# A two-layer sequence trunk on one Trainium2 core: the output gate moved into the final product, forget gates in pairs, GLA three slots earlier, weight sums on VectorE

## The reference, cut to what matters

```python
# x: (1, 2048, 1024) float32; layer 0 is S5 + sliding-window attention, layer 1 is gated linear attention (GLA)
# layer 0, end:
a_out = g * sigmoid(g @ w_glu + b_glu) * silu(g_a);  b_out = swa(q, k, v) * silu(g_b)
x = x + concat(a_out, b_out) @ ev_w_out
# layer 1:
h = rmsnorm(x, norm_w[1]);  q, k, v, r, a_lr = split(h @ od_w_in)          # 512, 512, 1024, 1024, 16 columns
log_a = log_sigmoid(a_lr @ w_a2 + b_a) / 16                                # the forget gates
o = gla(q, k, v, log_a)                                                    # 4 heads, chunks of 64, a state per head
c_out = rmsnorm_per_head(o) * norm_w * silu(r)                             # silu(r) is the output gate
x = x + c_out @ od_w_out;  return rmsnorm(x, final_norm)
```

## Time and profile before

| | us |
|---|---|
| median of 3 runs | 1678.32 (1676.89 to 1682.54) |
| the profiled execution, its own time | 1679.81 |
| its span, first to last instruction | 1677.7 |
| TensorE busy | 1598.3 (95%) |
| VectorE busy | 976.1 (58%) |
| ScalarE busy | 750.2 (45%) |
| GpSimd busy | 448.7 (27%) |
| mean granted TensorE clock | 0.987 |

### The profile page before, as it was taken

One profiled execution on the slowest core, in us unless ns is written; L12 is line 12 of the kernel. 1 busy time (PEld: TensorE's weight loads), 2 busy tenths in 40 slices (PEclk: granted clock), 3 DMA queues, 4 the chain that ended last, 5 costly groups with the idle time before them and its releaser, 6 DMA issues.

```text
span 1677.7 us, 23100 instructions
## 1 busy us (share of the span) xinstructions
PE 1598.3 (95%) x7626; PEld 1287.5 (77%) x7626; DVE 976.1 (58%) x1751; ACT 750.2 (45%) x1824; POOL 448.7 (27%) x646
## 2 busy tenths in 40 slices
PE   5999999999999989999889999996999999989998
PEld 4777788777777668888667888885788888868886
DVE  6744545667676563324476565777665666765443
ACT  6522334666666563334344343445443334442221
POOL 3883000000000341200275434345134343300110
PEclk9999999999999999999999999998999999999999
DMA  5566544455444766224367444355244343476663
GB/s 217 147 179 188 157 151 134 144 169 150 150 139 131 198 188 242 101 96 143 118 202 251 158 124 153 123 189 188 92 156 152 122 161 117 134 250 205 188 190 112
DMA packets 251388, 268.71 MB, mean 160 GB/s; under 512 B 53992, under 2 KB 186760, under 8 KB 251272
## 3 DMA queue, kind: packets, MB, share of 16 engines
q1 hardware_dynamic: 248616, 265.58, 50.5%
q10 hardware_dynamic: 2656, 1.67, 0.4%
HBM read 164.24 MB, written 102.96 MB: 159 GB/s over the span
## 4 chain that ended last, share of the span: by engine, by line
PE 71%; DVE 11%; ACT 5%; issue 5%; DMA 4%; POOL 3%; SPq 1%; DVEq 0%; ACTq 0%; POOLq 0%
PE bank L1225 22%; PE bank L2565 10%; PE bank L2623 10%; PE bank L2749 8%; PE score_banks L2565 4%; PE score_banks L2749 2%; DVE odd_stage L2300 2%; PE score_banks L1281 1%; DVE ht_lo L2242 1%; PE bank L1308 1%; DMA odd_gl_in<-scr_heads 1%; PE bank L1262 1%; DVE odd_w_lo_S L2242 1%; PE score_banks L2667 1%; PE bank L2689 1%
## 5 line engine op out<-in xcount | busy, mean ns | idle before, releaser
L1225 PE MATMUL bank<-ht_hi,ev_w_hi 128*128 128x512 f32 x576 | 239.9, 416 | 2.4 <-DVE ht_lo L937 2.4
L1225 PE MATMUL bank<-ht_hi,ev_w_lo 128*128 128x512 f32 x576 | 226.8, 394 | 0.0
L1225 PE MATMUL bank<-ht_lo,ev_w_hi 128*128 128x512 f32 x576 | 226.6, 393 | 0.0
L1225 PEld LDWEIGHTS bank<-ht_hi,ev_w_hi 128*128 128x128 f32 x576 | 109.0, 189 | 38.7 <-issue 17.1
L1225 PEld LDWEIGHTS bank<-ht_lo,ev_w_hi 128*128 128x128 f32 x576 | 108.9, 189 | 24.9
L2565 PE MATMUL bank<-ht_hi 128*128 128x512 f32 x288 | 120.1, 417 | 5.8 <-issue 5.8
L1225 PEld LDWEIGHTS bank<-ht_hi,ev_w_lo 128*128 128x128 f32 x576 | 109.2, 190 | 19.6
L712 POOL TENSOR_TENSOR ht_lo_raw<-ht_lo_raw,glu_g_first 128x512 f32<-128x512 f32 x4 | 6.4, 1642 | 415.9 <-DMA ht_lo_raw<-scr_gate_a 409.7
L2565 PE MATMUL bank<-ht_lo,ht_hi 128*128 128x512 f32 x288 | 113.2, 393 | 0.0
L2565 PE MATMUL bank<-ht_hi,ht_lo 128*128 128x512 f32 x288 | 112.7, 391 | 0.0
L2135 ACT ACTIVATE odd_gl_o<-bank 128x256 f32<-128x256 f32 x64 | 24.7, 385 | 168.6 <-DVE odd_gl_state L2361 156.0
(11 more groups left out here) (374 smaller groups left out, 4263.4 us busy)
## 6 DMA issues: line engine op xcount, KB each, us to landing
odd_w_raw<-od_w_in SPq DMA_DIRECT2D x24, 1024.0 KB, 5.8
odd_gl_in<-scr_heads SPq DMA_DIRECT2D x32, 640.0 KB, 4.8
scr_heads<-odd_stage SPq DMA_DIRECT2D x64, 256.0 KB, 6.4
ev_w_raw<-ev_w_in SPq DMA_DIRECT2D x17, 512.0 KB, 6.0
ev_s_cos_sin<-scr_s_cos_sin SPq DMA_DIRECT2D x32, 256.0 KB
odd_xo_sum<-x SPq DMA_DIRECT2D x16, 512.0 KB, 4.7
scr_x<-odd_xo_sum SPq DMA_DIRECT2D x16, 512.0 KB, 3.0
scr_gla_mix<-odd_gl_out SPq DMA_DIRECT2D x32, 256.0 KB, 2.3
```

Of the source, the lines that this page charges most:

```text
L1225: mm = pe.matmul(acc[n % 3], w[j][:, k, :], h[:, k, t], start=(k == 0 and r == 0), stop=(k == KT - 1 and r == 2))
```

## The change

The silu of r leaves the slots: its columns are stored raw, and the gate is formed in the final product, for each tile two tanh of 128x512 on ScalarE into free PSUM banks, and two more operations on VectorE behind the present one. GLA starts three slots earlier in both halves, forget gates come two in a slot. The sums of the weights move to VectorE, as do the subtractions of T3 and T4 in the middle. At the seam between the layers and in the GLU stage loads, casts and waits are reordered.

```diff
-    GLA_AT = (17, 64)
-    GATE_AT = (4, 51)
+    GLA_AT = (14, 61)
+    GATE_AT = (3, 51)
-        return [8 * half + s - at_ for half, at_ in enumerate(GATE_AT) if 0 <= s - at_ < 8]
+        return [8 * half + 2 * (s - at_) + n for half, at_ in enumerate(GATE_AT) if 0 <= s - at_ < 4 for n in range(2)]
+    m_th = [(bank[6], bank[7]), (bank[2], bank[3])]
...
     def sync(sp):
             if i == 0:                      # load_x4; in the change "if i == 1"
                 sp.wait_ge(hb_summed, 4 * N_TB)
-        load_att(0)
         load_wo(0)
         load_wo(1)
...
         load_wo(2)
         load_g(3)
+        load_att(0)
...
-            for k in gates_at(s - 2):
+            for k in gates_at(s - 1):
...
     def gpsimd(pool):
         gate_g(1)
         gate_g(2)
-        gate_att(0)
         gate_g(3)
+        gate_att(0)
...
-        for o in S_ORDER:
-            weight_sum(0, o)
-            if it + 1 < N_IT:
-                for o in {1: ("S1", "S2", "S4"), 2: ("S3",)}.get(j, ()):
-                    weight_sum(it + 1, o)
-            for o in H_SPLIT_AT.get(s, ()):
-                if o in H_LO_POOL:
-                    lower_second(o)
...
     def scalar(act):
-            if i == 11:
+            if i == 13:
                 upper_att(0)
-            if i in (5, 7, 9, 11, 13):
-                upper_wo((i - 5) // 2)
+            if i in (6, 8, 10, 12, 14):
+                upper_wo((i - 6) // 2)
...
         for m in range(NT):
+            if m == NT - 1:
+                split(0, "A11")
             if m:
                 upper_out(m - 1)
             if m == NT - 1:
-                split(0, "A11")
+                split(0, "S2")
...
+        def mix_tanh(t):
+            act.wait_ge(mix_in[j], mix_in_0[j] + 32 * (t // 2 + 1))
+            (waits for the last GLA work at t = 0 and 1, for mul_done of tile t - 2 later)
+            for h in range(2):
+                s.activation(m_th[j][h], m_sil[j][:, 4 * h:4 * h + 4], ACT.Tanh, scale=0.5).then_inc(tanh_done, 1)
...
-            (silu_tanh of four roles in the slots of is_r)
+            if s_ == 94: mix_tanh(0)
+            if s_ == 95: split_mix(0)
+            if s_ == 96: mix_tanh(1)
+            (in the final loop: if t + 2 < NT: mix_tanh(t + 2), ahead of the squares)
...
     def vector(dve):
-            if i == 12:
+            if i == 14:
                 lower_att(0)
-            if i in (6, 8, 10, 12, 14):
-                lower_wo((i - 6) // 2)
+            if i in (7, 9, 11, 13, 15):
+                lower_wo((i - 7) // 2)
...
         split(0, "A11")
+        dve.wait_ge(wo_free, wo_free_0 + 2)
+        weight_sum(0, "S1"); weight_sum(0, "S2"); weight_sum(0, "S4")
         residual(NT - 1)
         sum_first("T4")
+        split(0, "S2")
         lower_first("T2")
         normed_out(NT - 1)
-        split(0, "S2")
-        lower_first("B21")
+        weight_sum(0, "S3")
         split(0, "A12")
         split(0, "S3")
+        lower_first("B21")
         lower_first("T4")
...
         def gated(t):
-            v.scalar_tensor_tensor(m_on[j][:], m_on[j][:], 0.5, m_sil[j][:], ALU.mult, ALU.mult).then_inc(mul_done, 1)
+            (the same, then_inc(half_done, 1); then for each half h, when its tanh is done:)
+                rows = m_on[j][:, 4 * h:4 * h + 4]
+                v.scalar_tensor_tensor(rows, m_th[j][h], 1.0, rows, ALU.add, ALU.mult)    # the last one: mul_done
...
             (slots: gate_log now ahead of advance; silu gone; prepare(0) waits for hb_summed)
             if step(s + 1) is not None:
                 mask(step(s + 1))
+            if it + 1 < N_IT:
+                for o in {1: ("S1", "S2", "S4"), 2: ("S3",)}.get(j, ()):
+                    weight_sum(it + 1, o)
             for o in W_SPLIT_AT[j]:
                 (split)
             for o in H_SPLIT_AT.get(s, ()):
-                if o in H_LO_DVE:
-                    lower_second(o)
+                lower_second(o)
...
     def tensor(pe):                         # out_products
             if m % 4 == 0:
                 pe.wait_ge(mix_lo_done, 4 * GLU_AT.index(m // 4) + 4)
-                pe.wait_ge(att_lo_done, m // 4 + 1)
...
+                if m % 4 == 0 and k == 4:
+                    pe.wait_ge(att_lo_done, m // 4 + 1)
```

More of the change, by code:

```diff
@@ L1483, in gates_output_odd @@
     turned_at = (raw_hi[:, 0:4, cols(1)], raw_hi[:, 4:8, cols(1)])
-    tb_in = [at(f"hb_in{j}", (20, 4)[j], [P, 4, BLK // 2]) for j in range(2)]
+    tb_in = [at(f"hb_in{j}", (20, 6)[j], [P, 4, BLK // 2]) for j in range(2)]
     tb_out = [at(f"hb_out{j}", 24 + 4 * j, [P, 4, BLK // 2]) for j in range(2)]
@@ L1800, in sync @@
             before = it - 1
-            if j == 3 and it < N_IT and not is_r(it):
+            if j == 3 and it < N_IT:
                 store_out(it, "C11")
             if j == 0 and before >= 0:
-                for role in (("C11",) if is_r(before) else ("C21", "C22")):
-                    store_out(before, role)
+                store_out(before, "C21")
+                store_out(before, "C22")
             if j == 1 and before >= 0:
-                store_out(before, "C22" if is_r(before) else "C12")
-            if j == 2 and is_r(before) and s < N_SLOT:
-                store_out(before, "C21")
                 store_out(before, "C12")
@@ L1878, in gpsimd @@
         gate_g(2)
+        gate_g(3)
         gate_att(0)
-        gate_g(3)
-        for m in range(NT):
+        for m in range(NT - 1):
             inverse_out(m)
@@ L2242, in split, with weight_sum @@
             v.tensor_tensor(w_lo[o], w_from[o], w_hi[o].bitcast(F32), ALU.subtract).then_inc(w_ready, 1)
+        def weight_sum(i, o):
+            prev = i - 1
+            if o == "S1":
+                dve.wait_ge(w_in[i % 2], 16 * (i // 2 + 1))
+                if i:
+                    dve.wait_ge(w_ready, w_ready_0 + 1 + w_no(prev, "S1"))
+                v.tensor_tensor(w_from["S1"], w_from["A21"], w_from["A22"], ALU.add).then_inc(s_added, 1)
+            if o == "S2":
+                if i:
+                    dve.wait_ge(p_done, product_no(prev, "S2"))
+                dve.wait_ge(s_added, s_no(i, "S1"))
+                v.tensor_tensor(w_from["S2"], w_from["S1"], w_from["A11"], ALU.subtract).then_inc(s_added, 1)
+            if o == "S4":
+                if i:
+                    dve.wait_ge(w_ready, w_ready_0 + 1 + w_no(prev, "S4"))
+                dve.wait_ge(s_added, s_no(i, "S2"))
+                v.tensor_tensor(w_from["S4"], w_from["A12"], w_from["S2"], ALU.subtract).then_inc(s_added, 1)
+            if o == "S3":
+                if i:
+                    dve.wait_ge(p_done, product_no(prev, "S3"))
+                v.tensor_tensor(w_from["S3"], w_from["A11"], w_from["A21"], ALU.subtract).then_inc(s_added, 1)
         def sum_first(o):
@@ L2300, in combine @@
             v.tensor_tensor(*ops, ALU.add).then_inc(ev_done, 1)
-        def silu(it, role):
-            dve.wait_ge(tanh_done, sil_no(it, role) + 1)
-            v.scalar_tensor_tensor(out_of[role], tanh[:], 1.0, out_of[role], ALU.add, ALU.mult).then_inc(sil_done, 1)
         def gate_min(k):
@@ L2463, in gated @@
             dve.wait_ge(mix_in[j], mix_in_0[j] + 32 * (t // 2 + 1))
-            v.scalar_tensor_tensor(m_on[j][:], m_on[j][:], 0.5, m_sil[j][:], ALU.mult, ALU.mult).then_inc(mul_done, 1)
+            halved = v.scalar_tensor_tensor(m_on[j][:], m_on[j][:], 0.5, m_sil[j][:], ALU.mult, ALU.mult)
+            halved.then_inc(half_done, 1)
+            dve.wait_ge(half_done, t + 1)
+            for h in range(2):
+                dve.wait_ge(tanh_done, 2 * t + h + 1)
+                rows = m_on[j][:, 4 * h:4 * h + 4]
+                part = v.scalar_tensor_tensor(rows, m_th[j][h].rearrange("p (k t) -> p k t", k=4), 1.0, rows, ALU.add, ALU.mult)
+            part.then_inc(mul_done, 1)
         def lower(t):
@@ L2482, in vector @@
                         take_low(half, k)
+            for k in gates_at(s - 1):
+                gate_log(k)
             if s and step(s - 1) is not None:
@@ L2488, in vector @@
                 prepare(step(s + 2) // 2)
-            if j == 0 and is_r(it - 1):
-                silu(it - 1, "C22")
-            if j == 1 and is_r(it - 1):
-                silu(it - 1, "C21")
             if even(step(s + 3)):
@@ L2503, in vector @@
                     split(it + 1, o)
-            if j == 1 and is_r(it - 1):
-                silu(it - 1, "C12")
-            if j == 3 and is_r(it):
-                silu(it, "C11")
             if s == 1:
```

107 lines of the change are left out of this document (35 added, 72 removed).

## The result

The changed kernel takes 1662.55 us (median of six executions, 1659.37 to 1671.97), the one before beside it 1678.34: 15.8 us less, ratio 0.9903, 95% interval 0.9879 to 0.9927. The sign was right; the forecast was 1646, and 1662.55 lies just outside its range. Half of the 32 us did not come. The profiled execution took 1660.8 (span 1659.0).

The account below looks back on a forecast made before the run. TensorE, busy 95% of the span, was taken as the bound, with only idle and lower-clock time to win; 7.5 + 7.5 + 5.0 + 7.0 − 1.0 + 0.5 + 5.5 = 32 us gave 1646 us, range 1632 to 1662 (8 in 10).

Parts of the forecast that it names:

- The start of GLA waits on the first x4 load as before; 0.5 of 1.6. Bounds 0 and 1.6.: Start of GLA: TensorE's 1.6 us wait stays mostly as it was, with 0.5 us gained.
- The forget gates: Gates in pairs: TensorE waits 5.5 us against 4.6 for gate stores, a loss of 1 us; bounds −6 and +4.
- it0 to it5: First product matmul of iteration 0 to that of iteration 5 (rest of seam, gates, GLA start): forecast −5.4 us.
- The seam's second half: Seam between the layers, behind the first product: the 2.0 us wait on S2 goes, plus 2.3 of clock.
- The GLU stage: GLU stage: TensorE's 5.8 us wait for g goes, with half the clock's 3.4; 7.5 us gained, bounds 3 and 9.
- What is late next: `gate_g(3)` [...] and `gate_att(0)`: GLU stage: the operations late next; gate_att(0) is awaited only at the fifth k of the first out product.
- The middle: Slots 46 to 50: norm not awaited, no silu, but VectorE falls behind with the pieces; 7 us gained, bounds 2 and 15.
- The slots: Second half's slots: sums on VectorE cost nothing, VectorE reaches advance earlier, norm waits mostly go; 5.0 us, bounds 0 and 5.7.
- Shifting GLA by three slots also swaps which half has its exponentials in odd slots; I give that nothing: GLA in the slots: the swap of odd and even slots between the halves counted at nothing.
- rival (3): Slots: VectorE's sums hold up GLA, directly or through GpSimd's inverse, adding 64 us; 1722 us, chance 0.04.
- The last seam: Last seam and final product: GLA no longer reaches in, gated(0) starts at once; 5.5 us gained, bounds 2 and 8.
- Rival (1): Seams only: reordered seams and the end return 19.5 us, slots and middle give nothing; 1659 us, chance 0.17.

Follow-up runs that it names:

- run 5: Changed kernel with the store of C21 of iteration 13 issued ahead of the 1 MB load of weights in slot 56; 1654.2 us, ratio 0.9860.
- run 2: Changed kernel with the first GLA at slot 17 again and the first half's forget gates one in a slot (4 to 11); 1659.3 us, ratio 0.9885.
- run 1: Changed kernel with the first GLA beginning at slot 17 again instead of 14, the second staying at 61; 1669.5 us, ratio 0.9933.
- run 3: Changed kernel, GLA at (14, 61), with only one pair of forget gates in the first half and two in the second; 1658.9 us, ratio 0.9874.
- run 10: Changed kernel with the second x4 load of the first GLA issued ahead of the 1 MB load of weights in slot 12; 1656.3 us, ratio 0.9859.
- best_a: Changed kernel with GLA at (15, 61), single first-half gates in slots 3 to 10, and the edits of run 5 and run 7; 1650.6 us, ratio 0.9821.
- run 7: Changed kernel with GpSimd's first attention product (gate_att(0)) waiting until VectorE has made the last low part of g; 1658.9 us, ratio 0.9885.
- run 8: Kernel before with its output gate (tanh on ScalarE, product on VectorE) left out, raw products stored; 1669.5 us, ratio 0.9951.
- run 4: Changed kernel with the sums of weights S1 to S4 back on GpSimd in the places of the kernel before; 1666.5 us, ratio 0.9922.
- run 6: Changed kernel with the second GLA beginning at slot 62 instead of 61; 1660.5 us, ratio 0.9891.

## Why the prediction was half right

**The step that failed** is "The start of GLA waits on the first x4 load as before; 0.5 of 1.6. Bounds 0 and 1.6." With GLA three slots earlier, the load is not as before: in the second half its input is stored only one slot ahead of it, behind 1 MB of weights. I had priced GLA's shift as free, because I looked at what GLA collides with and not at what it needs. The second start came out 7.6 us above the forecast, of which run 5 gives back 5.7 by one reordered issue; some 1 us more is the paired gates (it13 to it15 took 42.1 us, 39.5 before, against 1.5 forecast). What is left of the 7.6, about 1 us, was not tried. At the first start the forecast 0.5 us did not come either: `first` waits 1.7 us there, 1.6 before.

**The forget gates** were mis-sized: −1 forecast, with −6 as the bound. The pairs cost 4.9 us in the first half alone (run 2 against 1, with GLA at 17) and some 1 us in the second, which is at the bound; with GLA at 14, where the start behind them waits too, all pairs but one are worth 1.6 us by the trace of run 3 (up to 4.3 by the spread). The cause named was right, two buffers whose stores must land: VectorE's rows show it waiting 2.56 and 1.08 us for them.

**it0 to it5** was 10.6 us worse in all. The two parts that were tested, the pairs (1.6 to 4.9 us) and the x4 load behind the weights (1.7 or somewhat more, run 10), are about half of it; `best_a`, with single gates and GLA one slot later, gives back 8.1. At the first start what TensorE gains ahead of it is waited for: run 2 reaches it3 13.7 us ahead of the kernel before and it5 only 8.0, with a 4.4 us wait in `first`. That the weights' and x4's transfers are what it then waits for is read from the traces (7.57 us in run 1); no run took them apart at this start. The seam's second half also returned less than 4.3: TensorE's wait for B22's low part grew from 0.8 to 2.6 us (3.5 with the sums on GpSimd, so they are not its cause), and one of 2.2 us for the low-rank rows came with the earlier gates.

**The GLU stage**: 6.9 us against 7.5 in the profiled trace, but not in each execution: two of nine traces lose nearly all of it to the meeting of run 7. Over the nine the stage takes 48.7 us on average, a gain of 5.0. "What is late next: `gate_g(3)` [...] and `gate_att(0)`" named the place and priced it at nothing. The Trainium skill (SBUF — State Buffer, Who interferes with whom) has the rule that a VectorE instruction with two SBUF inputs and a GpSimd instruction that reads SBUF exclude each other for the whole instruction; VectorE's 6.09 us beside GpSimd's 4.59 agree with it.

**The middle** gave 10.7 in place of 7, and for another reason in the main: 3.0 are the silu (80.4 to 77.4 us, run 8), 7.1 the earlier end of GLA (76.8 to 69.7, run 1 against the changed kernel), and T3, T4 and the rest have the 0.6 between. Two traces of one code differ by up to 1.6 us here. I had written that `norm` isn't awaited there, but gave it no term of its own.

**The slots** gave 5.7 in place of 5.0. The wait named (`norm`, 5.7 us) did go. But the path was another. Run 8 gives the silu 2.0 of it, and run 4 shows that the rest would have gone in the second half with the sums left on GpSimd, by the odd start, though GpSimd then stretches VectorE's A11 split to 1326 ns. So the freeing of VectorE is one of two ways to the same gain, and was credited with all of it: either the odd start (run 4) or the sums on VectorE (run 6) suffices. "Shifting GLA by three slots also swaps which half has its exponentials in odd slots; I give that nothing" was wrong. In the first half, now even, the sums on VectorE are what keeps 3.5 us from being lost. That they cost TensorE nothing in the slots was right, and rival (3), 1722 us, is refuted.

**The last seam** gave 7.1 against 5.5; run 6 shows that it hangs on the slot in which GLA ends, and the operations added to the final product cost nothing: 177.0 us from its first matmul to the last, 179.2 before.

Rival (1), 1659, came nearest in time and for the wrong reason: slots and middle did return theirs, and the starts of GLA took it. That the total lies so near the range is in part luck: the middle and the last seam returned 5.3 us more than forecast, against 18.2 lost at the two starts.

Three slips of the prediction's text change little. The terms it lists for the middle, 14.9 + 5.6 less 10 of waits and 2 to 3 of clock, make 7.5 to 8.5 and not 7. The 3.36 us piece isn't among rows 7; the trace has it at 1169.8 us. And the rival in which `inverse` is held up is (3), not the last.

## What to carry to other kernels

When a stage is moved earlier in a software pipeline, walk its input chain back to the last store that it reads, with the queue order and the landing times, before counting what it frees; here the gain of 7.1 us at one end of the first GLA and the loss at the start of the second came of the same edit. In a DMA queue that is worked off in order, issue a small transfer that something waits for ahead of a large one that has slack: one line was worth 5.7 us. Price a pipeline's phase (even or odd slot) before crediting the gain to the work that was moved to another engine. And look at how far two traces of one code differ in a stage before reading 2 us out of it.

## What was not expected of the hardware

One meeting of VectorE and GpSimd goes either way from execution to execution of one code. VectorE's subtraction, begun while GpSimd was in an instruction of 1.7 us, was done in 1.53 to 1.59 us in seven of nine traces, and GpSimd's next instruction then took 5.0 to 5.65 us; in the other two that one took 4.55 and 4.59 us, and VectorE's lasted 6.07 and 6.09 us. The GLU stage is some 6.4 us longer in those two. A gap in GpSimd's work isn't needed for VectorE to be first (four of the seven had none), and nothing in these traces tells beforehand which way it goes.

A 256 KB store issued 0.4 us behind a 1 MB load let its successor go 8.2 us later; issued ahead of that load, at most 4.3 us later (runs without and with the edit of run 5).
